# Keeping four projection halves in row slots so that one load serves both prompt tiles and the samples

## The reference, cut to what matters

```
h    = rmsnorm(x, norm1);  proj = h @ w_in              # 1024 -> q, k, v, o, u_pool (512 each) and 8 gates
mix  = [mLSTM(q, k, v, gates) * sigmoid(o), pool(u_pool)] @ w_out;  x += mix
q    = rmsnorm(x, norm2) @ peer_wq                      # 8 heads x 2 x 128
s    = q . sub_keys;  top 16 of each half, top 16 of the pair sums -> eidx, gate (per head)
x   += sum over the 128 chosen experts of gate * gelu(x_normed . u_tab[eidx]) * v_tab[eidx]
x   += sigmoid(x @ w_gate) * (p @ w_ple)
```

## Time and profile before

| What | us |
|---|---|
| median of three runs | 1671.47 (1671.4 to 1674.97) |
| the profiled execution's own time | 1673.4 |
| its span, first to last instruction | 1671.2 |
| PE busy | 1311.7 (78%) |
| DVE busy | 1013.2 (61%) |
| ACT busy | 704.7 (42%) |
| POOL busy | 499.7 (30%) |
| bytes moved by the DMA engines | 682.03 MB, 408 GB/s over the span |

### The profile page before, as it was taken

One profiled execution on the slowest core, in us unless ns is written; L12 is line 12 of the kernel. 1 busy time (PEld: TensorE's weight loads), 2 busy tenths in 40 slices (PEclk: granted clock), 3 DMA queues, 4 the chain that ended last, 5 costly groups with the idle time before them and its releaser, 6 DMA issues. The chain is left out here.

```text
span 1671.2 us, 19424 instructions
## 1 busy us (share of the span) xinstructions
PE 1311.7 (78%) x6310; PEld 495.1 (30%) x6310; DVE 1013.2 (61%) x2625; ACT 704.7 (42%) x1976; POOL 499.7 (30%) x532
## 2 busy tenths in 40 slices
PE   8978896788967798876676898668985776676677
PEld 4534343334412333321112344223441221111113
DVE  1468566846986336797555443855799654455454
ACT  3245554434344444334333464433343453333334
POOL 0032323322232123234333223323234333333330
PEclk9987998899988999997657999789997886676669
DMA  8699999999999999999999999999999999999994
GB/s 336 252 400 426 372 425 422 422 419 426 425 394 408 426 426 414 427 425 427 427 428 426 426 408 425 423 424 411 421 426 426 426 426 427 427 427 427 427 427 169
DMA packets 96018, 682.03 MB, mean 408 GB/s; under 512 B 11024, under 2 KB 12560, under 8 KB 14238
## 3 DMA queue, kind: packets, MB, share of 16 engines
q0 software_dynamic: 76032, 553.68, 79.1%
q1 hardware_dynamic: 19886, 127.12, 18.6%
HBM read 674.63 MB, written 6.59 MB: 408 GB/s over the span
## 5 line engine op out<-in xcount | busy, mean ns | idle before, releaser
L2172 DVE SCALAR_TENSOR_TENSOR rows<-rows,shown 128x1024 f32<-128x1024 f32 x528 | 637.5, 1220 | 499.2 <-DMA rows<-in_uv,index_B 270.0
L1294 PE MATMUL acc<-rows,weighted 128*64 128x512 f32 x2048 | 661.1, 753 | 213.9 <-ACT weighted L1697 208.6
L1503 POOL DMA_INDIRECT rows<-in_uv,index_A x256 | 242.9, 949 | 638.8 <-PE acc L1294 487.0
L981 PE MATMUL bank<-wring,turned 128*128 128x512 f32 (+1 forms) x832 | 384.7, 610 | 10.1 <-DMA wring<-in_w 8.1
L1503 POOL DMA_INDIRECT rows<-in_uv,index_B x256 | 241.6, 944 | 469.8 <-PE acc L1294 438.0
L1294 PEld LDWEIGHTS acc<-rows,weighted 128*64 128x64 f32 x2048 | 135.6, 158 | 644.4 <-ACT weighted L1697 490.5
L981 PEld LDWEIGHTS bank<-wring,turned 128*128 128x128 f32 x832 | 156.9, 197 | 195.4 <-issue 183.0
L1686 ACT ACTIVATE dots_B<-dots_B 128x1 f32<-128x1 f32 x256 | 51.8, 202 | 369.2 <-DVE rows L2172 360.2
L1686 ACT ACTIVATE dots_A<-dots_A 128x1 f32<-128x1 f32 x256 | 51.5, 201 | 318.6 <-DVE rows L2172 312.7
L1697 ACT ACTIVATE weighted<-consts,dots_A 128x64 f32<-128x64 f32 x256 | 89.0, 348 | 8.4
L1697 ACT ACTIVATE weighted<-consts,dots_B 128x64 f32<-128x64 f32 x256 | 89.0, 348 | 8.4
(11 more groups left out here) (315 smaller groups left out, 960.2 us busy)
## 6 DMA issues: line engine op xcount, KB each, us to landing
wring<-in_w SPq DMA_DIRECT2D x102, 1024.0 KB
out_sample<-scratch SPq DMA_DIRECT2D x2, 2128.5 KB
scratch<-in_c_s SPq DMA_DIRECT2D x2, 2064.0 KB, 15.8
rows<-in_uv,index_A POOLq DMA_INDIRECT x256
rows<-in_uv,index_B POOLq DMA_INDIRECT x256
keys<-in_keys SPq DMA_DIRECT2D x2, 1024.0 KB, 14.3
gain<-in_gain SPq DMA_DIRECT2D x3, 640.0 KB, 8.4
consts<-in_consts SPq DMA_DIRECT2D x1, 1243.0 KB, 10.9
```

The costliest lines, as they stand in the source:

```text
L981: ins = pe.matmul(ps[:, part], turned["A"][:, 4 * h + c, :], w[:, c, part], start=first, stop=end, skip_group_check=True)
L1294: ins = pe.matmul(acc[c * 64:(c + 1) * 64, :], weighted[:, n % STATS, :], row[:, c * BLOCK:(c + 1) * BLOCK], start=first, stop=end, skip_g ...
L1503: pool.indirect_dma_start(out=rows[:, n % RING, :], out_offset=None, in_=a["uv"], in_offset=bass.IndirectOffsetOnAxis(ap=index[kind][:, pa ...
L2172: dve.scalar_tensor_tensor(u, u, 1.0, shown[:, :, :], ALU.mult, ALU.mult, accum_out=dots[kind][:, part, i:i + 1]).then_inc(u_used, 1)
```

## The change

Four of the ten projection halves of layer 0, those of j = 3 (output gate) and j = 4 (pooling input), are loaded once, into row slots 4 to 7, and stay there until tiles 0, 1 and 2 have all used them. For that:

- SP loads the four during the opening, one each at the schedule's places of `project` (0,1,0), (0,1,1), (0,2,0) and (0,2,1), outside the ring of weight halves. The ring's own loads fall from 102 to 94: four are replaced by these, four (those of pass 1) are no longer made.
- `turn` and `norm` of tiles 1 and 2 move from the start of pass 1 into the opening: the two turns and tile 1's norm behind `pool_r` of tile 0, tile 2's norm behind the first `mix` half. Tile 1's transposed input goes into `xn["B"]`, which ACT's squaring also writes, so DVE waits for the square root first.
- The eight products `project` (1,3,h,t) and (1,4,h,t), t = 1, 2, move to just behind `query` (0,1,1), which itself is directly behind the first head's `turn_prob`, and so ahead of `turn_pq` and `match` of tile 0's second key block.
- Gathers 4 to 7 wait on POOL until tile 2 has used the half in their slot.
- x of tiles 1 and 2 is loaded at `project` (0,3,0) in place of (0,4,0); in layer 0 the sample states are loaded behind `project` (1,2,1,2) in place of (1,4,1,2).

```diff
+HELD = {("project", 0, j, h): 4 + 2 * (j - 3) + h for j in (3, 4) for h in range(2)}
+RELEASED = {slot: ("project", 1, key[2], key[3], 2) for key, slot in HELD.items()}
...
 def half_key(e):
+    if e[0] == "project" and e[1] == 1 and e[2] >= 3:
+        return ("project", 0, e[2], e[3])
...
 def make_schedule():
     first, second = stage_front(0), stage_front(1)
+    moved = [e for e in second if e[0] == "turn" or e[0] == "norm" and e[2] == "turn" or half_key(e) in HELD]
+    second = [e for e in second if e not in moved]
+    for after, group in ((("query", 0, 1, 1, 0), [e for e in moved if e[0] == "project"]),
+                         (("mix", 0, 0, 0, 0), [("norm", 2, "turn")]),
+                         (("pool_r", 0), [("turn", 1), ("turn", 2), ("norm", 1, "turn")])):
+        at = 1 + first.index(after)
+        first[at:at] = group
...
+        turned1 = {"A": turned["A"], "B": xn["B"][:, :].rearrange("p (c n) -> p c n", n=P), "S": turned["S"]}
...
             def half(e):
+                if e in HELD:
+                    pe.wait_ge(held_in[HELD[e]], 16)
+                    return rows[:, HELD[e], :].rearrange("p (c n) -> p c n", c=4)
...
+                elif key in HELD:
+                    if t == 2:
+                        ins.then_inc(held_used, 1)
...
+                if e in (("project", 0, 1, 0, 0), ("project", 0, 1, 1, 0), ("project", 0, 2, 0, 0), ("project", 0, 2, 1, 0)):
+                    key = ("project", 0, 2 + e[2], e[3])
+                    sp.dma_start(rows[:, HELD[key], :], a["w"][0, half_index(key)]).then_inc(held_in[HELD[key]], 16)
...
-                if e == ("project", 0, 4, 0, 0):
+                if e == ("project", 0, 3, 0, 0):
                     load_tiles()
-                if e[0] == "project" and e[2:4] == (4, 1) and KIND[e[4]] == "S":
+                if e in (("project", 1, 2, 1, 2), ("project", LAST, 4, 1, 5)):
                     layer = layer_of(e[4])
...
                 if kind != "S" and part == 0 and i % PER_HEAD == 0:
                     emptied(pool, "turn_index", t, batch_of("turn_index", t, i // PER_HEAD)[2])
+                if n in RELEASED:
+                    _, _, j, h, t2 = RELEASED[n]
+                    if h:
+                        b, k2 = use["project", t2, j]
+                        pool.wait_ge(bank_full[b], k2 + 1)
+                    else:
+                        pool.wait_ge(held_used, j - 2)
...
             def turn(t):
                 if t == 0:
                     dve.wait_ge(cols_in, 16)
-                turn_back("turn", t, 0)
+                if KIND[t] == "B":
+                    dve.wait_ge(root_ready, roots("turn", t, lanes=False))
+                turn_back("turn", t, 0, turned1[KIND[t]])
```

More of the change, by code:

```diff
@@ L488, in issue @@
             ready = self.known(n, "turn_index")
-            slot = self.finish_of(("vals", *GATHERS[n - RING])) if n >= RING else 0.0
+            slot = self.finish_of(("vals", *GATHERS[n - RING])) if n >= RING else self.ended.get((RELEASED[n], 0)) if n in RELEASED else 0.0
             if ready is None or slot is None:
@@ L521, in start_of @@
             waits.append(self.finish_of(("vals", *e[1:], EACH[KIND[t]] - 1)))
-        if stage in DENSE + ("embed",) and half_key(e) != APART:
+        if stage in DENSE + ("embed",) and half_key(e) != APART and half_key(e) not in HELD:
             n = self.halves.index(half_key(e)) if half_key(e) in self.halves else len(self.halves)
@@ L625, in commit @@
                 self.freed_at[use] = end
-        if engine == "PE" and e[0] in DENSE + ("embed",):
+        if engine == "PE" and e[0] in DENSE + ("embed",) and half_key(e) not in HELD:
             if half_key(e) not in self.halves:
@@ L723 @@
 for _e in SCHEDULE:
-    if _e[0] in ("project", "mix", "query", "gate", "embed"):
+    if _e[0] in ("project", "mix", "query", "gate", "embed") and half_key(_e) not in HELD:
         HALF_OF.setdefault(half_key(_e), len(HALF_OF))
@@ L727 @@
 LAST_USE = {HALF_OF[half_key(_e)]: _i for _i, _e in enumerate(SCHEDULE)
-            if _e[0] in ("project", "mix", "query", "gate", "embed")}
+            if _e[0] in ("project", "mix", "query", "gate", "embed") and half_key(_e) not in HELD}
 def gated(tile):
@@ L863, in build @@
         half_in = [sem(f"half_in{i}") for i in range(WRING)]
+        held_in = {slot: sem(f"held_in{slot}") for slot in HELD.values()}
+        held_used = sem("held_used")
         row_in = [sem(f"row_in{i}") for i in range(RING)]
@@ L960, in dense @@
             def dense(name, p, j, h, t, *sources):
-                w, kind = half(half_key((name, p, j, h))), KIND[t]
-                if j == 0:
+                key = half_key((name, p, j, h))
+                w, kind = half(key), KIND[t]
+                left = turned1[kind] if name == "project" else turned[kind]
+                if j == 0 or p == 1 and key in HELD:
                     for source in sources[h:h + 1]:
@@ L977, in dense @@
                         for g in range(4):
-                            ins = pe.matmul(ps[lane_group(g), 0:P], turned["S"][:, 4 * h + c, :], w[:, c, g * P:(g + 1) * P],
+                            ins = pe.matmul(ps[lane_group(g), 0:P], left[:, 4 * h + c, :], w[:, c, g * P:(g + 1) * P],
                                             start=first, stop=end, skip_group_check=True)
                     else:
-                        ins = pe.matmul(ps[:, part], turned["A"][:, 4 * h + c, :], w[:, c, part], start=first, stop=end,
+                        ins = pe.matmul(ps[:, part], left[:, 4 * h + c, :], w[:, c, part], start=first, stop=end,
                                         skip_group_check=True)
@@ L1021, in gates @@
                     else:
-                        ins = pe.matmul(ps[:, 0:8], turned["A"][:, c, :], w_gates[:, layer_of(t), c, :], start=first, stop=end)
+                        ins = pe.matmul(ps[:, 0:8], turned1[KIND[t]][:, c, :], w_gates[:, layer_of(t), c, :], start=first, stop=end)
                 closed(ins, "gates", t)
@@ L1554, in project @@
                 kind = KIND[t]
-                if j == 0:
+                if j == 0 or t in (1, 2):
                     act.wait_ge(inv_ready, roots("turn", t))
@@ L1757, in step, with turn_back @@
                 after(ins)
-            def turn_back(name, t, col):
+            def turn_back(name, t, col, dst):
                 m, n = ROWS[KIND[t]], 1 if KIND[t] == "S" else 2
@@ L1765, in turn_back @@
                     gains = cols[:, layer_of(t), col + i * c:col + (i + 1) * c]
-                    free(dve.tensor_tensor(turned[KIND[t]][:, i * c:(i + 1) * c, :],
+                    free(dve.tensor_tensor(dst[:, i * c:(i + 1) * c, :],
                                            ps[:, 0:c * m].rearrange("p (h c) -> p h c", h=c), across(gains, m), ALU.mult),
@@ L2015, in turn2 @@
             def turn2(t):
-                turn_back("turn2", t, 8)
+                turn_back("turn2", t, 8, turned[KIND[t]])
             def marked(ins):
```

## The result

| | before | after |
|---|---|---|
| median | 1673.22 us (1671.4 to 1677.47, 4 runs) | 1693.73 us (1691.71 to 1698.42, 4 runs) |
| ratio of the times | | 1.0129 (1.0109 to 1.0149) |
| profiled execution: its time, its span | 1673.4, 1671.2 | 1693.37, 1691.2 |

The change makes the kernel 1.3% slower. The prediction was 1670.6 us with a range of 1664 to 1677.5, so it was wrong in sign and by 23 us (1.8 of them because the median before, 1671.47 over three runs, is 1673.22 over four). I begin where the prediction began, with the page's DMA slices, and set them against the earlier trace rows.

The account below looks back on a forecast made before the run. The prediction took the sixteen DMA engines, full from 87 to 1643 us, as the bound. Its terms 1.7 + 10.7 - 9.8 - 3.5 = -0.9 us, against the median of 1671.47, gave 1670.6 us, range 1664 to 1677.5.

Parts of the forecast that it names:

- start, bytes and holes: Whole kernel: each edit priced by the full DMA stretch's start, the bytes in it and its holes.
- gather 0 later: Opening: ten more transposes and a small product on PE delay gather 0, +1.7 us, bounds +1.4 and +5.
- gathers 4 to 7: After the opening: DMA idles until moved products free the slots, gather 7 at 120.1; +10.7 us, bounds +2.6 and +13.
- bytes: Pass 1, inside the full DMA stretch: four halves of 1.049 MB no longer loaded, -9.8 us.
- head 2's index: Ahead of gather 16: index slips to near 143 but still arrives in time, 0 us, with 4 us of room.
- hole at 170: DMA hole at 170 to 175 us: taken as closed by the changed order, -3.5 us; other bound 0.
- rival 1: Opening: moved products run close together, `vals` afterwards, idle time 2.6 us; total 1662.5 to 1666; chance 0.29.
- a worse opening: Opening: unpriced slower outcome, sharing the 0.29 chance with tile 1's late ranking and the hole that stays.
- Rival 2: Transition to tile 1: its ranking comes too late for gather 128; 1676.6 to 1678.6; 0.29 with other slower cases.
- the releases on SP: SP's queue: earlier sample-state loads delay no `mix` half of pass 1, 0 us; one late half would cost 2.5.
- my three signs of being wrong: Gather 7 before 115 or behind 123; gather 0 moved over 3 us; new hole over 3 us behind 130.

Follow-up runs that it names:

- the rule tried in the kernel before: Kernel before, planned again with the accumulator copy (`place`) ahead of everything else that is ready: 1682.08 us, ratio 1.0043.
- the order by hand: Changed kernel with PE's list edited so moved products alternate with `vals`, the first samples product behind one `vals`: 1690.48 us, ratio 1.0112.
- packed: Changed kernel, but the planner puts the eight moved products ahead of everything else that is ready: 1680.98 us, ratio 1.0043.
- the kernel with one edit of PE's order: Kernel before with one tile 1 projection put behind `vals` of gather 22 on PE: 1670.78 us over twelve runs, ratio 0.9988.

## Why the prediction was wrong

The method held: start, bytes and holes account for 19.7 of the 20.0 us. Two things were not what I wrote.

| term | forecast | measured |
|---|---|---|
| gather 0 later | +1.7 | +1.9 (0.9 the change's, 1.0 a later start of the execution) |
| gathers 4 to 7 | +10.7 | +20.1 (22.0 - 1.9) |
| bytes | -9.8 | -9.8 |
| head 2's index | 0 | 0 (gather 16 waited 7.11 for it, until 156.52; engines full) |
| hole at 170 | -3.5 | -5.0 (135 to 300) |
| the order elsewhere | not in the sum | +10.9 (300 to 450), +1.5 in the rest |
| sum | -0.9 | +19.6 |

**The failed step is "Gathers 4 to 7".** The mechanism was right: idle engines, one release for each pair of products, `vals` in between. The size was wrong by 9.4 us, outside its upper bound of 13. I counted six `vals` as work of 1.01 us each, "that have become ready", and never asked in which order they stand ahead of the first samples product. Six there were. But from 93.71 to the end of the last product PE took 34.6 us, where my 18.6 + 2 + 6.1 make 26.7; its idle times in the rows above (0.53, 0.79, 1.49, 2.36), the lower clock (1.8) and 0.88 us of waiting for ACT at 116.95 make up the difference. A static order places `vals` by the planner's estimate, and the chip waits in place for each. Four of them stood ahead of the release of gather 4, so I should have worked out that release as well: it waits for the rows of gather 3. With an order near the one that I assumed, gather 7 goes out where I said. Even then the term was low: that kernel lacks 16.4 - 1.4 = 15.0 in the opening where I had 12.4 with the start, and no run separates the 2.6. The order of rival 1 lacks 11.7 where I had 4.3; there I had left out that gather 8 then waits for its index, which is 6.4. A lone gather took about as long as the 5.4 us that I assumed: gather 5 was issued at 116.37 and DVE had it at 121.91, 5.5 us. The Trainium skill's page "DMA: Bandwidth & Descriptors", section "Anatomy of one DMA", would make this 4.4 us, as an estimate; the trace shows more.

**What I left out: the whole order is made anew.** I treated the order behind 170 us as unchanged but for the moved work. It was made anew from end to end, and 10.9 us were lost where one copy on ACT fell behind five `dots`. A chance of 0.29 stood for a slower result. It named "a worse opening" without a price, and its mechanism was another: tile 1's own ranking was not late. Gather 128 goes out without a wait:

```profile
500.34 0.94 POOL L1535 DMA_INDIRECT rows<-in_uv,index_B  x1 [0.30 <-issue]
```

The dip at 475 to 515 is gone in exchange for the one at 525 to 535. Rival 2's mechanism is real all the same, as the rule tried in the kernel before shows.

**What was right.** The opening's extra work found its cover; PE waited for no held half in pass 0; the hole at 170 closed. That the releases on SP cost nothing fits the ledger, but no run tests it. The hole was larger than the 3.5 us that I read from the DMA share: by its 72 GB/s it lacked 4.2. Two of my three signs of being wrong came true: gather 7 behind 123 (128.60), and a new hole of over 3 us behind 130. Gather 0's 1.9 us against 1.7 was luck, as said above.

**Two slips that the result hides.** Of head 2's index I said that it would come near 143, with "4 us of room". It came at 156.52, and at 148.59 to 157.45 in the other traces in which four halves' products are moved and gather 16 waited for it. The term was 0 in the kernel after only because the engines were late themselves; with the opening shortened by hand the index was the bound. And the lower end of my own range adds up to 1.4 + 8.4 - 9.8 - 3.5 = -3.5, not -4.

**What is shown and what is not.** Shown: the wait on the held slots is some 20 us of the opening (3.8 missing where nothing is held and all else moved); the order of PE sets its size (21.8 to 23.5 missing in four traces of the planned order, 16.4 and 17.6 in two of the order by hand); and the copy's place costs 6 to 9 us (6.3 by the ledger, 7.5 by the ratios, 9.0 by the medians, against the kernel that differs in nothing else). No version with a held half beat the kernel before; the best of them, one half held, is at 1.0040. Not shown: that no order could make the change pay. Seven kernels with four halves held were run, the fastest, packed, at 1.0043. Its ledger rather speaks for trying on: apart from gather 8's wait the four halves cost it 13.1 - 6.4 - 3.8 = 2.9 us, an estimate, and they save 9.8. No order was run that keeps the products together and still brings head 1's index in time. Open: why three re-planned kernels with nothing held (1.0026, 1.0048, 1.0043) each lose at other places. It fits that the order before was an exceptionally good one among many close ones, but no run tells whether that is so.

## What to carry to other kernels

Data that sits in a ring's slots is paid for in time to release: take the instruction that frees each slot, read everything ahead of it in its engine's actual order, and ask of each what it waits for; above all whether it waits for the ring itself. Here a half cost 4.9 us of idle engines and saved 2.46. PE needed 4.64 us for the pair of products that frees what DMA refills in 2.46, and that difference of 2.2 is less than half of the 4.9; the rest came from what stood in between. When a planner writes the order, every change is a new order everywhere: compare the two orders at each switch of accumulators and at each tile's first index before you price anything, and leave some microseconds for what that brings (4 to 8 here, with nothing held). Keep a ledger of missing transfer time by stretch; it showed both places in one view. And measure a shift from a fixed instruction to the next, not from the start of the execution, before you call it the change's.

## What was not expected of the hardware

The times of one kernel, the hand-ordered opening, spread over 0.8% (1684.75, 1687.39, 1693.57, 1697.61) at mean clocks of 0.844 to 0.854; the twelve of the kernel with one edit of PE's order lie within 0.5%. No run tells why. The lower clock came at the worst moment: it left the releasing product at 1.94 us in place of 1.08. Whether the wait brought it on is not shown. From 105 to 110 us the clock was 0.50 in the kernel after and 1.00 in the packed order and the one by hand, but it was 0.50 too in the kernel that only moves the turns, and 0.53 in the kernel before with one edit further on, and neither of these holds a slot.
